# A token norm's shift carried by the first scatter of each layer, and half of its gain moved to GpSimd

## The chip, the cores and the metric

The kernel runs on one core of one Trainium2 chip. The metric is the device time of one execution in microseconds. The engines go by the names of the profile: PE is TensorE (PEld its weight loads), DVE is VectorE, ACT is ScalarE, POOL is GpSimd, SP is SyncE, which here only issues DMAs. An engine's name with a q behind it is its sequencer.

## The reference

Two layers, each with four token mixers, a projection, a norm, a mixture of 16 experts with two experts for each token, and a second norm. There are 256 tokens of 2048 values; everything is float32. What the change touches is the path from the first norm of a layer to the sum over the experts:

```python
h = layer_norm(DN_ALPHA * h + mix, ln1_g[l], ln1_b[l])
ffn = hier_moe(h, w_rg[l], b_rg[l], w_re[l], b_re[l], w_gate[l], w_up[l], w_down[l])
h = layer_norm(DN_ALPHA * h + ffn, ln2_g[l], ln2_b[l])

...
for e in range(N_EXPERTS):
    h = jax.nn.silu(xt @ w_gate[e]) * (xt @ w_up[e])
    out = out + combine[:, e:e + 1] * (h @ w_down[e])
```

The loop stands in `hier_moe`, where `xt` is `h` as 256 x 2048. `combine` is zero for all but the two experts that the router picks for a token, so only those have to be computed.

## The kernel before

The tokens lie in SBUF as `h`, 128 partitions by two halves (`h[:, 0]`, `h[:, 1]`) by 2048. After the output projection VectorE normalises each half without gain and shift. TensorE turns it and computes the router's logits; gain and shift are folded into the router's weights there. Then VectorE picks the experts for each token, counts the tokens of each expert, and gives every expert one or more blocks of 32 token places (BLK). Experts are sorted by their number of blocks, the fixed first two (FIXED) ahead; the sorted table goes as whole numbers into `tabi`, from which each engine loads registers to set its loops. The part for the first two experts is written first, and signalled as `tab_first`; the rest follows later, as `tab_ready`.

A block runs so. VectorE makes `hot`, a matrix that marks which token fills which place (function `mark`; for the first block it signals `first_hot`). TensorE gathers the rows of `h_k`, a copy of the normalised tokens that ScalarE made (`hk_ready`), and turns them (L1010); VectorE applies gain and shift in `take_rows` and signals `xe_ready`. TensorE multiplies with the gate and up weights (L1038). ScalarE and VectorE form the hidden values (`sgate`, `hidden`), TensorE turns them and multiplies with the down weights (L1056). The result `yraw` is scattered back onto the tokens by a product with `place`, a matrix of 0 and combine weight (L1021, `scatter`), and VectorE adds the scattered banks to `h` (`add_block`). The scatter of a block is done one block later: in block g TensorE scatters block g - 1, four banks for the first half of the tokens, behind the gather of the next block, and four for the second half behind the first half of the down products. It may write a bank again only when VectorE has added it. So the first block of a layer has a scatter with nothing to carry: `place` is set to zero for it (L1576), and it adds zeros.

Since `h` holds the normalised tokens until the gather has its copy, VectorE multiplies both halves by the gain (L1555, L1556, signal `gain_done`) between the first `mark` and the table, and adds the shift to both (L1581, L1582) before the loop over the blocks. Gain and shift come as `gb`, each vector broadcast to 128 partitions by SyncE, 1 MB each, once the mixed heads are split (`mix_split`); they end as the signal `gb1_loaded`. The rows that say where each token goes, `rows`, lie over the gain in memory, so ScalarE's copy into `rows` (L714) waits for `gain_done`.

Behind these two loads SyncE issues the expert weights: six units of 2 MB for an expert (four of gate and up, two of down), into nine slots of SBUF. A unit from the tenth on waits until the unit that held its slot has been used: `gu_quarter` after a quarter of the gate and up products of the last block of an expert, `gu_done`, `y_half` and `y_done` after the others. Unit 12 also waits for `tab_ready`. Each engine runs its instructions in the order in which they stand; nothing is rescheduled. GpSimd has no work between the entry norm's gain and shift (L489, L492, on `h`, while the mixers run) and the next layer.

In memory `area(48, ...)` begins with `yraw` (2 KB), `place` and `place_2` (1 KB each) and `rows` (4 KB).

Of the kernel before, what the change touches and what calls it, by code (L numbers as in the profile page):

```python
# [14 lines left out]
P = 128  # L15
BLK = 32
# [29 lines left out]
def trunk(nc, x, ln0_g, ln0_b, w_in, conv_a_w, conv_a_b, lru_wa, lru_ba, lru_wx, lru_bx, lru_lam, conv_b_w,  # L46
# [27 lines left out]
    with ctx:  # L74
# [67 lines left out]
        gb = area(48, 2 * D).rearrange("p (m n) -> p m n", m=2)  # L142
# [65 lines left out]
        table_by = yraw.rearrange("p (r e n) -> p r e n", r=2, e=16)  # L208
# [79 lines left out]
        gain_done, hk_ready = signal("gain_done", 1), signal("hk_ready", NT)  # L288
# [38 lines left out]
        def _(eng):  # L327
# [48 lines left out]
            for l in range(L):  # L376
# [20 lines left out]
                for m, v in enumerate((ln1_g, ln1_b)):  # L397
                    eng.dma_start(gb[:, m, :], v[l:l + 1].to_broadcast([P, D])).then_inc(gb1_loaded.sem, 16)
# [58 lines left out]
        def _(eng):  # L457
# [36 lines left out]
            for l in range(L):  # L494

                eng.wait_ge(xnT_done, (l + 1) * 8)
                eng.memset(c_scT, 0.0).then_inc(sc_zero.sem, 1)

                eng.wait_ge(bias_loaded.sem, bias_loaded.at(l, 16))
                eng.memset(blocks(a_H, HEADS)[0:CH, :, 0:CH], NEG).then_inc(mask_ready.sem, 1)  # L500
                eng.wait_ge(gb_in_loaded, 32 * (l + 1))
                eng.wait_ge(w_used.sem, w_used.at(l, 21))
                affine(gb_in)


        @block.scalar
        def _(eng):
# [55 lines left out]
            for l in range(L):  # L563
# [148 lines left out]
                eng.wait_ge(gain_done.sem, gain_done.at(l, 1))  # L712
# [393 lines left out]
        def _(eng):  # L1106
# [104 lines left out]
            for l in range(L):  # L1211
# [343 lines left out]
                tt(h[:, 0, :], h[:, 0, :], gb[:, 0, :], ALU.mult)  # L1555
                tt(h[:, 1, :], h[:, 1, :], gb[:, 0, :], ALU.mult).then_inc(gain_done.sem, 1)  # L1556
# [9 lines left out]
                for r0, r1 in ((0, 2), (2, 3)):  # L1566
                    n = r1 - r0
                    tt(table_by[:, 0:n], tab[:, r0:r1].rearrange("p r (o e) -> p r o e", o=1).to_broadcast([P, n, 16, 16]),
                       sorted_by.rearrange("p (o n) e -> p o n e", o=1).to_broadcast([P, n, 16, 16]), ALU.mult)
                    eng.drain()  # L1570
                    eng.tensor_reduce(tabf[:, r0:r1], table_by[:, 0:n], AX.X, ALU.add)
                    eng.drain()
                eng.tensor_copy(tabi[:, 0:3, FIXED:], tabf[:, :, FIXED:])
                tt(tabi[:, 3, FIXED:], tabf[:, 0, FIXED:], tabf[:, 1, FIXED:], ALU.add).then_inc(tab_ready.sem, 1)
                eng.wait_ge(spread_ready.sem, spread_ready.at(l, 1))
                eng.memset(place, 0.0).then_inc(place_ready, 1)  # L1576
# [3 lines left out]
                tt(h[:, 0, :], h[:, 0, :], gb[:, 1, :], ALU.add)  # L1580
                tt(h[:, 1, :], h[:, 1, :], gb[:, 1, :], ALU.add)  # L1581
# [69 lines left out]
```

## Time and profile before

| | us |
|---|---|
| median of 3 runs | 1740.17 (1737.57 to 1743.55) |
| the profiled execution, its time | 1737.94 |
| the profiled execution, its span | 1736.2 |
| TensorE busy | 1578.6 (91%) |
| VectorE busy | 922.2 (53%) |
| ScalarE busy | 522.3 (30%) |
| GpSimd busy | 48.8 (3%) |
| mean DMA rate | 315 GB/s |

The span is what the profiler covers, from the first to the last instruction of one execution; the time of that execution is 1.7 us longer. A layer takes about half of the span: some 410 us of mixers and router, then some 450 us of experts. The page gives busy time and, in slices, how it is spread; a timeline gives the start and length of each instruction and, in brackets, how long its engine stood idle before it and what ended that. Windows give the busy time of each engine between two moments, in the order PE, PEld, DVE, ACT, POOL, with the granted clock of TensorE as a share of 2.4 GHz, the share of time in which the DMA engines were busy, and GB/s. Most of VectorE's instructions come through two helpers and so have the line L1108 or L1111.

### The profile page before, as it was taken

What the parts mean: (1) busy time and instruction counts of PE and PEld (TensorE: products, weight loads), DVE (VectorE), ACT (ScalarE), POOL (GpSimd) and SP (SyncE); (2) the same over time, 40 slices, a digit from 0 to 9 for tenths busy, and PEclk for the clock granted to TensorE, in tenths of its full rate; (3) what the DMA queues carried; (4) which work ended last, traced back from release to release, by engine and by line L of the source; (5) the groups of instructions that cost most, each with busy time, mean ns of one, the idle gap of its engine ahead of it and who ended that gap; (6) DMA issues with size and microseconds to landing.
All of it is one profiled execution on the core that took longest, in us unless ns stands there. A gap on an engine that the chain in (4) does not pass through costs nothing.

```text
span 1736.2 us, 35349 instructions
## 1 busy us (share of the span) xinstructions
PE 1578.6 (91%) x14820; PEld 1067.3 (61%) x14821; DVE 922.2 (53%) x1443; ACT 522.3 (30%) x600; POOL 48.8 (3%) x34
## 2 busy tenths in 40 slices
PE   8999999997999999956699999999989999996664
PEld 8999899884444444322299999998754444432221
DVE  7657655646455555422467476455465455543234
ACT  4553453323121121110264543543232121211011
POOL 0004000000000000000000050000000000000000
PEclk9999999999999999988899999999989999998887
DMA  9554455588999999999965545555989999999996
GB/s 309 196 168 136 153 169 192 194 334 365 421 422 422 418 419 399 423 422 422 409 211 181 161 142 170 174 174 192 421 338 420 422 422 421 408 423 421 423 421 270
DMA packets 139206, 547.28 MB, mean 315 GB/s; under 512 B 23060, under 2 KB 26360, under 8 KB 88568
## 3 DMA queue, kind: packets, MB, share of 16 engines
q1 hardware_dynamic: 138740, 546.13, 80.7%
q8 instruction: 57, 0.93, 0.2%
q14 instruction: 21, 0.17, 0.0%
q10 hardware_dynamic: 388, 0.04, 0.0%
HBM read 544.04 MB, written 2.10 MB: 315 GB/s over the span
## 4 chain that ended last, share of the span: by engine, by line
PE 74%; SPq 15%; DMA 4%; DVE 3%; issue 2%; DVEq 1%; ACT 1%; ACTq 0%
PE ps L798 24%; PE ps L1038 14%; PE ps L955 10%; SPq L430 9%; PE ps L1056 7%; SPq L434 5%; PE ps L795 5%; PE ps L1021 4%; PE ps L1002 3%; DMA room<-in_w_down_dram 3%; PE ps L1010 1%; DVE room L1108 1%; DVE h L1108 1%; PE ps L874 0%; DMA h<-in_x_dram 0%
## 5 line engine op out<-in xcount | busy, mean ns | idle before, releaser
L1038 PE MATMUL ps<-room 128*32 128x256 f32 x6016 | 374.4, 407 | 95.7 <-DMA room<-in_w_up_dram 90.3
L1108 DVE TENSOR_TENSOR w_lo<-room,w_hi 128x2048 fp32r<-128x2048 f32 x120 | 276.8, 2316 | 237.3 <-ACT w_hi L513 236.8
L1038 PEld LDWEIGHTS ps<-room 128*32 128x32 f32 x6016 | 202.3, 116 | 283.0 <-DMA room<-in_w_up_dram 110.4
L798 PE MATMUL ps<-hT_hi,w_hi 128*128 128x256 f32 x1152 | 330.2, 287 | 1.6 <-DVE hT_lo L1108 1.6
L798 PE MATMUL ps<-hT_hi,w_lo 128*128 128x256 f32 x1152 | 327.2, 284 | 0.0
L798 PE MATMUL ps<-hT_lo,w_hi 128*128 128x256 f32 x1152 | 327.1, 284 | 0.0
L513 ACT ACTIVATE w_hi<-room 128x2048 fp32r<-128x2048 f32 x120 | 228.3, 1914 | 228.1 <-PE ps L798 103.8
L1108 DVE TENSOR_TENSOR h<-h,ps 128x512 f32<-128x512 f32 x376 | 232.7, 680 | 98.3 <-PE ps L1021 97.8
L798 PEld LDWEIGHTS ps<-hT_hi,w_hi 128*128 128x128 f32 x1152 | 222.4, 193 | 4.4 <-DVE hT_lo L1108 2.0
L798 PEld LDWEIGHTS ps<-hT_hi,w_lo 128*128 128x128 f32 x1152 | 222.4, 193 | 0.7 <-issue 0.5
L798 PEld LDWEIGHTS ps<-hT_lo,w_hi 128*128 128x128 f32 x1152 | 222.3, 193 | 0.0
L1108 DVE TENSOR_TENSOR room<-room,ps 128x128 f32<-128x128 f32 (+2 forms) x53 | 18.5, 352 | 368.4 <-ACT room L720 363.0
L1056 PE MATMUL ps<-room 128*32 128x512 f32 x1504 | 184.3, 608 | 10.8 <-DMA room<-in_w_down_dram 10.8
L709 ACT ACTIVATE room<-ps 128x512 f32<-128x512 f32 (+1 forms) x143 | 70.4, 492 | 369.1 <-PE ps L1056 261.0
L720 ACT ACTIVATE room<-ps 128x128 f32<-128x128 f32 x47 | 13.0, 277 | 367.1 <-PE ps L1038 367.1
L1021 PE MATMUL ps<-room 32*128 32x512 f32 x752 | 115.0, 642 | 6.5 <-DVE h L1108 5.3
L1056 PEld LDWEIGHTS ps<-room 128*32 128x32 f32 x1504 | 39.7, 110 | 114.0 <-issue 86.3
L955 PE MATMUL ps<-w_hi,mix_hi 128*128 128x512 f32 x256 | 100.0, 391 | 0.0
L955 PE MATMUL ps<-w_lo,mix_hi 128*128 128x512 f32 x256 | 99.6, 389 | 0.0
L955 PE MATMUL ps<-w_hi,mix_lo 128*128 128x512 f32 x256 | 99.6, 389 | 0.0
L1002 PE MATMUL ps<-room 128*32 128x512 f32 x784 | 94.4, 599 | 2.5 <-DVE room L1108 2.5
L1021 PEld LDWEIGHTS ps<-room 32*128 32x128 f32 x752 | 34.0, 182 | 87.4 <-DVE h L1108 46.7
(246 smaller groups left out, 1421.3 us busy)
## 6 DMA issues: line engine op xcount, KB each, us to landing
room<-in_w_gate_dram SPq DMA_DIRECT2D x128, 1024.0 KB, 18.2
room<-in_w_up_dram SPq DMA_DIRECT2D x128, 1024.0 KB, 20.2
room<-in_w_down_dram SPq DMA_DIRECT2D x128, 1024.0 KB, 15.7
room<-in_w_in_dram SPq DMA_DIRECT2D x88, 1024.0 KB, 5.0
room<-in_w_out_dram SPq DMA_DIRECT2D x32, 1024.0 KB, 5.0
room<-in_ln_g_dram SPq DMA_DIRECT2D x5, 1024.0 KB, 5.6
room<-in_ln_b_dram SPq DMA_DIRECT2D x5, 1024.0 KB, 8.0
h<-in_x_dram SPq DMA_DIRECT2D x4, 512.0 KB, 6.3
```

Of the source, the lines that this page charges most:

```text
L430: eng.dma_start(unit_gu(u)[:, m], src[:, 4 * i:4 * i + 4, :]).then_inc(unit_loaded[u % SLOTS], 16)
L434: eng.dma_start(unit_down(u)[:, f, :], src[:, 2 * (i - 4) + f, :]).then_inc(unit_loaded[u % SLOTS], 16)
L513: eng.activation(w_hi[n % 4][:], w_raw(n % UNITS), ACT.Copy).then_inc(w_rounded.sem, 1)
L709: eng.activation(dst, ps[:, b, 0:dst.shape[1]], ACT.Copy).then_inc(ready, 1)
L795: last = eng.matmul(ps[:, b + o, :], x_[:, kk, o * P:o * P + P], w_, start=opens, stop=ends)
L798: last = eng.matmul(ps[:, b + o // 2, (o % 2) * T:(o % 2) * T + T], w_[:, o * P:o * P + P], x_[:, kk, :], start=opens and o % 2 == 0, stop ...
L955: last = eng.matmul(ps[:, b + t, :], m[:, k, t * P:t * P + P], w, start=(q == 0 and k == 0 and j == 0), stop=(q == 3 and k == 3 and j == 2))
L1002: last = eng.matmul(ps[r0:r0 + BLK, 3, :], hot[:, t, :], h_k[:, t, 4 * c:4 * c + 4, :], start=(t == 0), stop=(t == NT - 1), tile_position= ...
L1021: eng.matmul(ps[:, 4 + c, :], place[r0:r0 + BLK, t * P:t * P + P], yraw[r0:r0 + BLK, :], start=True, stop=True, tile_position=(r0, 0)).the ...
L1038: last = eng.matmul(ps[r0:r0 + BLK, 0, 0:2 * P], xe[:, x0:x0 + BLK], unit_gu(u)[:, :, k, c * P:c * P + P], start=(i == 0 and k == 0), stop ...
L1056: last = eng.matmul(ps[r0:r0 + BLK, 2, :], hmT[:, BLK * f:BLK * f + BLK], unit_down(u)[:, f % 2, c * 512:c * 512 + 512], start=(f == 0), s ...
L1108: return eng.tensor_tensor(o, a, b, op)
```

## The change

In each layer:

- `gb` becomes `gain_1`, the gain alone, and lies elsewhere (area 56). The shift is no longer broadcast: it is loaded as four rows of 512 values into `yraw`, at partitions 0, 32, 64 and 96, after GpSimd has set `yraw` to zero (signal `yraw_zero`). SyncE waits for that before it issues the load.
- `place` is set by VectorE to 1 where the partition's number within its 32 is 0 (`slot_of`), and 0 elsewhere, in place of zeros throughout. So the first scatter adds the shift to every token, and the two adds of the shift on VectorE go.
- The gain of `h[:, 1]` moves from VectorE to GpSimd, which waits for `gb1_loaded`, `hk_ready` and `first_hot`. `gain_done` now comes from GpSimd, and VectorE waits for it before the loop. ScalarE's copy into `rows` no longer waits for it.
- `place` is set right behind the gain of `h[:, 0]`, so the wait for `spread_ready` (that copy's signal) moves ahead of the table. The table's scratch is now `place_2`, half as large, so its three rows are computed one by one and not two and one.

The diff, cut; behind the two lines of memory come SyncE's part, GpSimd's, ScalarE's and VectorE's:

```diff
-        gb = area(48, 2 * D).rearrange("p (m n) -> p m n", m=2)
+        gain_1 = area(56, D)
...
-        table_by = yraw.rearrange("p (r e n) -> p r e n", r=2, e=16)
+        table_by = place_2.rearrange("p (r e n) -> p r e n", r=1, e=16)
...
                 eng.wait_ge(mix_split.sem, mix_split.at(l, 4))
-                for m, v in enumerate((ln1_g, ln1_b)):
-                    eng.dma_start(gb[:, m, :], v[l:l + 1].to_broadcast([P, D])).then_inc(gb1_loaded.sem, 16)
+                eng.dma_start(gain_1, ln1_g[l:l + 1].to_broadcast([P, D])).then_inc(gb1_loaded.sem, 16)
+
+                eng.wait_ge(yraw_zero.sem, yraw_zero.at(l, 1))
+                eng.dma_start(yraw[0:P:BLK, :], ln1_b[l].rearrange("(c n) -> c n", c=4)).then_inc(gb1_loaded.sem, 16)
...
                 affine(gb_in)
+                eng.wait_ge(mix_split.sem, mix_split.at(l, 4))
+                eng.memset(yraw, 0.0).then_inc(yraw_zero.sem, 1)
+
+                eng.wait_ge(gb1_loaded.sem, gb1_loaded.at(l, 32))
+                eng.wait_ge(hk_ready.sem, hk_ready.at(l, NT))
+                eng.wait_ge(first_hot.sem, first_hot.at(l, 1))
+                eng.tensor_tensor(h[:, 1, :], h[:, 1, :], gain_1, ALU.mult).then_inc(gain_done.sem, 1)
...
-                eng.wait_ge(gain_done.sem, gain_done.at(l, 1))
                 eng.wait_ge(spread_done.sem, spread_done.at(l, 1))
...
-                tt(h[:, 0, :], h[:, 0, :], gb[:, 0, :], ALU.mult)
-                tt(h[:, 1, :], h[:, 1, :], gb[:, 0, :], ALU.mult).then_inc(gain_done.sem, 1)
+                tt(h[:, 0, :], h[:, 0, :], gain_1, ALU.mult)
+                eng.wait_ge(spread_ready.sem, spread_ready.at(l, 1))
+
+                ts(place, slot_of[:].to_broadcast([P, T]), 0.0, None, ALU.is_equal).then_inc(place_ready, 1)
...
-                for r0, r1 in ((0, 2), (2, 3)):
+                for r0, r1 in ((0, 1), (1, 2), (2, 3)):
...
-                eng.wait_ge(spread_ready.sem, spread_ready.at(l, 1))
-                eng.memset(place, 0.0).then_inc(place_ready, 1)
...
-                tt(h[:, 0, :], h[:, 0, :], gb[:, 1, :], ALU.add)
-                tt(h[:, 1, :], h[:, 1, :], gb[:, 1, :], ALU.add)
+                eng.wait_ge(gain_done.sem, gain_done.at(l, 1))
```

On GpSimd, in the first layer from the clearing of `c_scT` for the mixers to the same instruction of the second layer; before:

```order
L497 MEMSET room 128x1024 [waits xnT_done]
L500 MEMSET room 64x4x64 [waits bias_loaded]
L489 TENSOR_TENSOR h<-h,room 128x2048 [waits w_used,gb_in_loaded]
L489 TENSOR_TENSOR h<-h,room 128x2048
L492 TENSOR_TENSOR h<-h,room 128x2048 x2
L497 MEMSET room 128x1024 [waits xnT_done]
```

and of the changed kernel:

```order
L499 MEMSET room 128x1024 [waits xnT_done]
L502 MEMSET room 64x4x64 [waits bias_loaded]
L491 TENSOR_TENSOR h<-h,room 128x2048 [waits w_used,gb_in_loaded]
L491 TENSOR_TENSOR h<-h,room 128x2048
L494 TENSOR_TENSOR h<-h,room 128x2048 x2
L507 MEMSET room 128x512 [waits mix_split]
L512 TENSOR_TENSOR h<-h,room 128x2048 [waits first_hot,hk_ready,gb1_loaded]
L499 MEMSET room 128x1024 [waits xnT_done]
```

Two instructions are new there, and the second is released by VectorE's `first_hot`.

On VectorE, from the gain to the table's end in the first layer (`room` is the memory in which nearly all tiles lie, `place` and the table among them); before:

```order
L1108 TENSOR_TENSOR h<-h,room 128x2048 [waits hk_ready,gb1_loaded]
L1108 TENSOR_TENSOR h<-h,room 128x2048
L1557 COPY room<-slot_of 128x1
L1108 TENSOR_TENSOR carry<-carry,room 128x1
L1560 TENSOR_REDUCE room<-room 128x16
L1561 COPY room<-iota 128x16
L1108 TENSOR_TENSOR room<-room,iota 128x256
L1108 TENSOR_TENSOR room<-room 128x512
L1571 TENSOR_REDUCE room<-room 128x32
L1108 TENSOR_TENSOR room<-room 128x256
L1571 TENSOR_REDUCE room<-room 128x16
```

and of the changed kernel:

```order
L1116 TENSOR_TENSOR h<-h,room 128x2048 [waits hk_ready,gb1_loaded]
L1119 TENSOR_SCALAR room<-slot_of 128x256 [waits spread_ready]
L1567 COPY room<-slot_of 128x1
L1116 TENSOR_TENSOR carry<-carry,room 128x1
L1570 TENSOR_REDUCE room<-room 128x16
L1571 COPY room<-iota 128x16
L1116 TENSOR_TENSOR room<-room,iota 128x256
L1116 TENSOR_TENSOR room<-room 128x256
L1581 TENSOR_REDUCE room<-room 128x16
L1116 TENSOR_TENSOR room<-room 128x256
L1581 TENSOR_REDUCE room<-room 128x16
```

The second gain has become the small instruction that makes `place`, and the table's pair of instructions of 512 has become two pairs of 256; one more pair of 256 follows in the changed kernel.

Further on, from the table's end to the loop's first add; before:

```order
L1573 CAST tabi<-room 128x3x14
L1108 TENSOR_TENSOR tabi<-room 128x14
L1576 MEMSET room 128x256 [waits spread_ready]
L309 TENSOR_LOAD tabi [waits tab_first]
L309 ISA x2
L309 TENSOR_LOAD tabi
L309 ISA x2
L1539 REGISTER_ALU
L1108 TENSOR_TENSOR room<-room,ps 128x128 [waits sg_ready]
L1108 TENSOR_TENSOR h<-h,room 128x2048 x2
L1583 UNCONDITIONAL_BRANCH
```

and of the changed kernel:

```order
L1583 CAST tabi<-room 128x3x14
L1116 TENSOR_TENSOR tabi<-room 128x14
L309 TENSOR_LOAD tabi [waits tab_first]
L309 ISA x2
L309 TENSOR_LOAD tabi
L309 ISA x2
L1547 REGISTER_ALU
L1116 TENSOR_TENSOR room<-room,ps 128x128 [waits sg_ready]
L1590 UNCONDITIONAL_BRANCH [waits gain_done]
```

The two adds of 128x2048 and the memset are gone, and the wait for `gain_done` stands where the adds stood.

## Rows read from the trace of the kernel before

**Rows 1.** Page, parts 1 and 2: TensorE's busy time; DMA in 40 slices.
```profile
PE 1578.6 (91%) x14820; PEld 1067.3 (61%) x14821; DVE 922.2 (53%) x1443; ACT 522.3 (30%) x600; POOL 48.8 (3%) x34
...
GB/s 309 196 168 136 153 169 192 194 334 365 421 422 422 418 419 399 423 422 422 409 211 181 161 142 170 174 174 192 421 338 420 422 422 421 408 423 421 423 421 270
```

**Rows 2.** Windows of the expert stages; last columns clock, DMA share, GB/s.
```profile
420.00:590.00 170.00, 165.17 (x2055) 71.89 (x2047) 92.32 (x197) 33.79 (x55) 0.00 (x0) 0.98 1.01 421
590.00:700.00 110.00, 109.09 (x1400) 47.69 (x1398) 59.63 (x131) 21.22 (x35) 0.00 (x0) 1.00 1.00 411
700.00:850.00 150.00, 103.45 (x1137) 41.15 (x1137) 46.68 (x103) 17.04 (x27) 0.00 (x0) 0.89 1.01 422
1280.00:1450.00 170.00, 165.21 (x2027) 70.97 (x2023) 92.54 (x196) 31.64 (x54) 0.00 (x0) 0.98 1.01 421
1450.00:1530.00 80.00, 79.15 (x1021) 34.70 (x1017) 44.31 (x96) 16.63 (x27) 0.00 (x0) 1.00 1.01 415
```

**Rows 3.** Windows of two holes; SyncE's issue that ends the first.
```profile
413.00:418.00 5.00, 4.49 (x60) 3.58 (x64) 3.50 (x6) 0.46 (x1) 0.00 (x0) 1.00 0.14 54
...
690.00:692.00 2.00, 2.00 (x44) 1.23 (x40) 0.40 (x3) 0.00 (x0) 0.00 (x0) 1.00 0.64 147
...
417.88 0.33 SPq L430 DMA_DIRECT2D room<-in_w_gate_dram  x1
```

**Rows 4.** Timelines around first_hot: start, duration, engine, instruction; PEldq: register loads.
```profile
410.51 0.22 DVE L1108 TENSOR_TENSOR room<-hot 128x64 f32<-128x64 f32 x1
...
410.90 0.24 DVE L1111 TENSOR_SCALAR room<-room,carry 128x16 f32<-128x16 f32 x1
...
411.36 0.16 DVE L1108 TENSOR_TENSOR tabi<-room 128x2 int32<-128x2 f32 x1
...
411.50 0.15 DVE L1507 SCALAR_TENSOR_TENSOR tabi<-room,carry 128x1 int32<-128x1 f32 x1
...
L309 PEldq SEQ_ASSERT  x2: 18/21/24, 412.5 to 413.1; - x2
...
413.51 0.66 PE L1010 MATMUL ps<-ident,room 128*128 128x128 f32 x4 [0.71 <-ACT room L709]
...
415.89 7.11 PE L1038 MATMUL ps<-room 128*32 128x256 f32 x128
...
1270.24 0.66 PE L1010 MATMUL ps<-ident,room 128*128 128x128 f32 x4 [0.71 <-ACT room L709]
```

**Rows 5.** Timelines of the first block; last row from the chain.
```profile
416.40 4.49 DVE L1108 TENSOR_TENSOR h<-h,room 128x2048 f32<-128x2048 f32 x2
...
426.49 4.49 DVE L1108 TENSOR_TENSOR h<-h,room 128x2048 f32<-128x2048 f32 x2
...
431.99 3.60 PE L1021 MATMUL ps<-room 32*128 32x512 f32 x8 [2.74 <-DVE h L1108]
...
439.16 7.83 PE ps L1038 x128
```

**Rows 6.** VectorE beside GpSimd, timelines; first two groups of instructions (ns).
```profile
L1108 DVE TENSOR_TENSOR w_lo<-room,w_hi 128x2048 fp32r<-128x2048 f32 x120 | 276.8, 2316 | 237.3 <-ACT w_hi L513 236.8
...
L489 POOL TENSOR_TENSOR h<-h,room x4: 4506/5024/5559, 152.7 to 1012.5; 128x2048 f32<-128x2048 f32 x4
...
154.40 3.88 DVE L1310 SCALAR_TENSOR_TENSOR room<-room 128x1024 f32<-128x1024 f32 x1
...
162.84 4.61 POOL L492 TENSOR_TENSOR h<-h,room 128x2048 f32<-128x2048 f32 x1
...
163.70 5.90 DVE L1108 TENSOR_TENSOR w_lo<-room,w_hi 128x2048 fp32r<-128x2048 f32 x1 [5.41 <-ACT w_hi L513]
```

**Rows 7.** Windows at the lower clock; an idle stretch, timeline.
```profile
434.00:440.00 6.00, 6.00 (x31) 1.46 (x33) 5.20 (x13) 0.75 (x2) 0.00 (x0) 0.51 1.02 423
1291.00:1297.00 6.00, 6.00 (x35) 1.42 (x36) 4.95 (x13) 1.01 (x2) 0.00 (x0) 0.50 1.01 418
...
397.95 2.07 PE L924 MATMUL ps<-ident,h 128*128 128x128 f32 x16 [2.18 <-DVE h L1111]
```

More of the change, by code:

```diff
@@ L287, in trunk @@
             signal(n, 1) for n in ("logits_done", "ex_in", "ex_ready", "m_ready", "ranks_done", "tab_ready"))
-        gain_done, hk_ready = signal("gain_done", 1), signal("hk_ready", NT)
+        yraw_zero, gain_done, hk_ready = signal("yraw_zero", 1), signal("gain_done", 1), signal("hk_ready", NT)
         spread_done, spread_ready, wts_ready = (signal(n, 1) for n in ("spread_done", "spread_ready", "wts_ready"))
```

## The prediction

> **What bounds the kernel now.** I read the page first, in 40 slices: TensorE is busy nearly everywhere, and DMA moves about 420 GB/s through the two long expert stretches (slices 11 to 20 and 31 to 39) [rows 1]. The windows of these stretches say more. From 420 to 590 us, and again from 700 to 850, the DMA engines deliver 421 and 422 GB/s without a hole, while TensorE is 97% and 69% busy; between them, from 590 to 700, they deliver 411 [rows 2]. The second layer shows the same: 421, then 415 between 1450 and 1530. So the expert stage is bound by the stream of weights. Its length is the moment at which the stream restarts, plus the bytes, plus the holes in the stream. I look for what moves the restart, and what fills the holes.
>
> *The restart.* From 413 to 418 us DMA is all but idle (54 GB/s) [rows 3]: all nine slots are full, and the next load waits until the first expert's first quarter of gate and up products releases one. SyncE issues it at 417.88 [rows 3]. TensorE begins these products at 415.89 [rows 4]. A microsecond that this start slips is a microsecond of the DMA bound stage.
>
> *The holes.* At 690 to 692 us DMA is down to 147 GB/s [rows 3]. In this part an expert has two blocks of tokens and TensorE takes a little longer for one than the stream does, so slots come free late. Holes in the first layer: (422 - 411) / 422 x 110 us = 2.9 us. In the second: (422 - 415) / 422 x 80 us = 1.3 us. Together 4.2 us. That is all that an earlier TensorE can win in both layers: after 700 us it waits for weights anyway.
>
> **What the change takes away.** After the first gate and up products VectorE has two gains (416.40, 4.49 us) and later two shifts (426.49, 4.49 us), 2.25 us each; TensorE's second scatter of the first block waits for the adds behind them, until 431.99, idle for 2.74 us [rows 5]. Afterwards TensorE runs at the lower of its two clocks, granted 0.51 from 434 to 440 us [rows 7]. The change removes both shifts and one gain from VectorE. Count from G, the start of the gate and up products (415.89 before [rows 4]). The product of the hidden layer, just ahead of the shifts, ended at 426.5, G + 10.6 [rows 5]. It comes 2.25 us sooner for the gain, and about 0.5 us later for the third pair of small instructions that the table now takes: G + 8.9; the mask of ones costs what the zeros cost. The loop's first four adds then wait for the first scatter alone and end, by an estimate of 0.7 us each, at about G + 12.1. TensorE stood before its second scatter at 431.99 - 2.74 = 429.25, G + 13.4; it gets there at G + 12.9, as its first scatter no longer waits half a microsecond for the mask behind the table. No wait is left. The second scatter (1.1 us) and the second half of the down products (1.9 us, half of what they take at the low clock) end at G + 15.9, where the second expert begins, instead of at G + 23.3 (439.16): 7.4 us earlier, of which 2.7 us is the wait and most of the rest the low clock.
>
> *How much arrives.* The next weights cap it. Units of 2 MB land 5 us apart from the restart on; counted so, the third expert has to wait some 2 us for its last down unit, and TensorE's lead over the stream is then about 5.6 us. That still exceeds the holes of either layer. I book the holes as filled: **-4.2 us**, and no more. The copy of the rows on ScalarE no longer waits for the gain: worth nothing by itself, as the mask is wanted only at G + 2.8. The megabyte less of broadcast shift is 2.4 us of DMA time ahead of a 5 us hole: nothing. The clearing of yraw on GpSimd is due when the mixed heads are split, long before SyncE's last load of projection weights; SyncE does not wait for it: nothing, at most 1 us, and that too before the hole.
>
> **What the change adds: GpSimd's gain, at a bad place.** GpSimd gets the factor for h[:, 1] as soon as first_hot is signalled, at 410.73. What do the two engines do to one another when both read two tiles from SBUF? The trace has the pair, where GpSimd applies the entry norm: its four products of this size take 4.51 us at the least and 5.56 at the most, and VectorE's scalar_tensor_tensor of 128x1024, issued at 154.40 in their midst, takes 3.88 us. VectorE's subtraction at 163.70 takes 5.90 us where the mean of its 120 fellows is 2.32: it ends at 169.60, just 2.15 us after GpSimd's instruction that began at 162.84 and took 4.61 ended (167.45) [rows 6]. So an instruction of either waits until the other's is over, whole, and the two don't share.
>
> Here VectorE has small work on the path at that time: the number of blocks of the first experts, written to tabi. At 411.36 comes a tensor_tensor of 128x2 with two SBUF operands [rows 4], two instructions short of tab_first at about 411.65. GpSimd starts at about 410.9 and holds to 410.9 + 4.5 = 415.4. tab_first then comes 0.3 us behind (if only the tensor_tensor is held) or 0.75 us behind (if the tensor_scalar at 410.90 is held too): 415.7 to 416.1, 4.0 to 4.5 us late. Behind it stand, on TensorE, two register loads (from tab_first to 413.1) [rows 4], and then the turning of the first rows, which began at 413.51 when ScalarE's copy released it: there 0.4 us of slack. So the turning starts at 417.1 to 417.6, and G with it 3.6 to 4.1 us later. I take 3.8. In the second layer the turning began at 1270.24 [rows 4] with 0.5 us of slack and slightly faster loads: 3.3 to 3.8, I take 3.5. Sum **+7.3 us**, all of it ahead of the restart. VectorE's own gain comes after GpSimd has finished, and gain_done is long there when the loop wants it.
>
> The Trainium skill has this as a rule ("SBUF — State Buffer", Who interferes with whom): the port pair shared by VectorE and GpSimd is an exclusive lock held for the whole instruction, and a VectorE instruction with two SBUF inputs contends with a GpSimd one that reads SBUF; the trace agrees, with its 5.90 us. The page adds that a tensor_scalar or a cast can take the pair in its two-port mode, by which the later end of my bracket would hold (0.45 us a layer more); that instructions of a few elements are held no run here shows yet.
>
> **The clock.** TensorE would idle from 412.8, the gather's end, to about 417.3, 4.5 us (before, 0.71 us stood here [rows 4]). The idle stretch of 2.74 us at the first scatter was followed by 6 us at half clock, and in the second layer there is the same fall at the same place [rows 5, 7]; an idle stretch of 2.18 us at 396 us was not followed by one. I expect the lower clock here in both layers, over the first quarter at least: 7.11 us for 128 products is 1.8 us a quarter, twice that at half clock, so 1.8 us a layer, **+3.6 us**. From below this is 0; from above it is half of 6.6 us of low clock, 3.3 us a layer. The later fall at 434 us goes, as its idle stretch goes; that is in the 7.4 us above.
>
> **Sum.** 7.3 + 3.6 - 4.2 = +6.7 us. The profiled execution took 1737.94 us, with a span of 1736.2; it would become 1744.6. The median of the three runs, 1740.17, is 2.2 us above it, and on that I forecast **1747 us**, 0.4% slower.
>
> **Rivals.**
> A, the forecast: held, low clock, holes filled. 1747 (1744 to 1751).
> B, held, but the clock stays at 2.4 GHz as it did at 396 us: 7.3 - 4.2 = +3.1, 1743.
> C, the other side: VectorE's small instructions slip through, or GpSimd starts only after 411.6. All rows of a hold concern 1024 elements and more. Then G stays and the holes are filled: -4.2, 1736. The point from which it decides is a hold of 2.1 us a layer: below it the change gains.
> D, held, and the holes stay, since the lower clock and the late landings eat the lead: 7.3 + 3.6 = +10.9, 1751.
> E, half a hold, since GpSimd has to wait its turn and finds VectorE between two instructions: about 0, 1740.
>
> **Chances.** A 0.50, B 0.20, C 0.14, D 0.08, E 0.08. A measurement of this kernel tells about 0.3% from no change, 5.2 us, so slower means above 1745.4 and faster below 1735.0. Slower: 0.40 of A, 0.03 of B, all of D: 0.51. Faster: 0.06 of C and 0.01 of E: 0.07. Within: 0.42. The range from 1738 to 1752 leaves out most of C below (0.11) and 0.05 above; the likeliest case's own is 1744 to 1751.
>
> **What would show it.** In the timeline after: GpSimd's product from about 410.9 for 4.5 us; VectorE's tensor_tensor on tabi lasting about 4 us instead of 0.16; the gate and up products from about 419.7 instead of 415.9; DMA idle for about 9 us, not 5; a granted clock near 0.5 in the quarter before the restart; no wait of TensorE at the second scatter; no hole between 590 and 700 us, and 422 GB/s there. I am wrong if tabi's instruction stays at 0.16 us (then C), or if the window from 590 to 700 still has 411 GB/s (then D).

## The result, and the profile after

The changed kernel takes 1745.76 us, the kernel before 1739.67 (medians of 13 runs each). The ratio is 1.0041, with a 95% interval of 1.0031 to 1.0052: slower by 0.4%. One run of the changed kernel (2250.70 us) and one of the kernel with 1024 columns further on (3902.77 us) stood far off from all others and count in no ratio. The profiled execution took 1745.64 us, its span is 1743.6, 7.4 us above the one before.

The page of the changed kernel, against [rows 1]:

```profile
PE 1575.7 (90%) x14820; PEld 1067.6 (61%) x14821; DVE 918.6 (53%) x1441; ACT 522.3 (30%) x600; POOL 58.8 (3%) x38
...
GB/s 308 195 178 130 164 174 175 193 343 282 421 421 422 421 422 416 422 422 421 408 201 179 170 140 161 168 188 194 385 311 421 422 422 421 422 422 422 422 422 276
```

The stream looks as before but for the slices at its restart (365 GB/s is now 282 in the first layer, 421 and 338 are now 385 and 311 in the second). The windows of the late part of each expert stage, against [rows 2] (the last number is GB/s):

```profile
590.00:700.00 110.00, 109.09 (x1403) 47.80 (x1395) 58.03 (x127) 21.50 (x36) 0.00 (x0) 1.00 1.01 419
...
1450.00:1530.00 80.00, 79.72 (x1016) 34.75 (x1009) 41.81 (x92) 16.04 (x28) 0.00 (x0) 1.00 1.01 422
```

The stream has 419 GB/s where it had 411, and in the second layer 422 where it had 415. The holes are filled, the first layer's not wholly: (422 - 419) / 422 x 110 us = 0.8 us is left. So the change brings nearly all that it could bring, and the loss comes from elsewhere. VectorE around first_hot, against [rows 4]:

```profile
411.34 0.17 DVE L1119 TENSOR_SCALAR room<-room 128x32 f32<-128x32 f32 x1
411.59 4.56 DVE L1119 TENSOR_SCALAR room<-room,carry 128x16 f32<-128x16 f32 x1
...
416.38 0.16 DVE L1116 TENSOR_TENSOR tabi<-room 128x2 int32<-128x2 f32 x1
...
416.51 0.15 DVE L1515 SCALAR_TENSOR_TENSOR tabi<-room,carry 128x1 int32<-128x1 f32 x1
```

and GpSimd in the same place:

```profile
411.60 4.53 POOL L512 TENSOR_TENSOR h<-h,room 128x2048 f32<-128x2048 f32 x1 [104.61 <-DVE room L1116]
```

VectorE's tensor_scalar of 16 elements, 0.24 us before, takes 4.56 us: it begins with GpSimd's product of 4.53 us and ends with it. tab_first is signalled behind the instruction at 416.51. TensorE and SyncE then:

```profile
418.39 1.11 PE L1018 MATMUL ps<-ident,room 128*128 128x128 f32 x4 [4.89 <-issue]
419.29 2.87 PE L1081 MATMUL ps<-ident,room 128*128 128x128 f32 x16
422.09 7.11 PE L1046 MATMUL ps<-room 128*32 128x256 f32 x128
...
434.47 1.20 PE L1029 MATMUL ps<-room 32*128 32x512 f32 x8
...
437.68 7.11 PE L1046 MATMUL ps<-room 128*32 128x256 f32 x128 [0.16 <-issue]
```

```profile
424.08 0.34 SPq L432 DMA_DIRECT2D room<-in_w_gate_dram  x1
```

TensorE stands idle for 4.89 us before it turns the first rows, for which it stood 0.71 us before. The gate and up products begin at 422.09, and the first weight is issued at 424.08. At the second scatter (434.47) it no longer waits. The granted clock (the column before DMA share) over the turning and the spreading of the places, in both layers:

```profile
418.00:421.00 3.00, 2.61 (x13) 2.62 (x13) 1.39 (x3) 0.00 (x0) 0.00 (x0) 0.50 0.02 5
...
1278.00:1281.00 3.00, 3.00 (x14) 3.00 (x15) 1.72 (x4) 0.00 (x0) 0.00 (x0) 0.50 0.03 5
```

From here on I count from the end of first_hot's instruction on VectorE, since that moment itself moves between executions (see the end). Restart is SyncE's first issue of a weight after the hole.

| from first_hot, us | before, layer 1 / 2 | changed, layer 1 / 2 |
|---|---|---|
| turning of the first rows | 2.78 / 2.77 | 6.96 / 6.58 |
| gate and up products (G) | 5.16 / 5.15 | 10.66 / 10.55 |
| restart of the stream | 7.15 / 7.14 | 12.65 / 12.54 |
| second expert, from the restart | 21.1 / 21.1 | 13.6 / 13.7 |
| last scatter of the stage | 449.4 / 448.2 | 452.6 / 452.7 |

The last scatter is TensorE's last instruction of an expert stage; before, and of the changed kernel, in both layers:

```profile
860.16 2.33 PE L1096 MATMUL ps<-room 32*128 32x512 f32 x16 [0.80 <-ACT room L709]
...
1715.67 2.32 PE L1096 MATMUL ps<-room 32*128 32x512 f32 x16 [0.80 <-ACT room L709]
```

```profile
864.06 2.32 PE L1104 MATMUL ps<-room 32*128 32x512 f32 x16 [0.80 <-ACT room L718]
...
1724.09 2.32 PE L1104 MATMUL ps<-room 32*128 32x512 f32 x16 [0.80 <-ACT room L718]
```

The stream restarts 5.5 and 5.4 us later. Less the filled holes, 2.1 and 1.3 us by the windows, that should leave 3.4 and 4.1 us; the stages are longer by 3.2 and 4.5. The 7.4 us between the spans are these two, 0.7 us by which first_hot itself came later in the first layer, and 1.0 us by which the second layer's last stretch, behind the last scatter, was shorter (19.5 against 20.5 us).

### The profile page after: what moved, and what is told of

The parts are those of the page before. It is cut to its first block, busy times and chain, and to the rows that moved or that the text cites. A ratio compares the mean times of both kernels' runs of the same rounds, so it can differ in the third digit from the quotient of the medians.

```text
span 1743.6 us, 35355 instructions
## 1 busy us (share of the span) xinstructions
PE 1575.7 (90%) x14820; PEld 1067.6 (61%) x14821; DVE 918.6 (53%) x1441; ACT 522.3 (30%) x600; POOL 58.8 (3%) x38
## 4 chain that ended last, share of the span: by engine, by line
PE 74%; SPq 14%; DMA 6%; DVE 3%; issue 2%; ACT 1%; DVEq 0%; ACTq 0%
PE ps L806 24%; PE ps L1046 14%; PE ps L963 10%; SPq L432 9%; PE ps L1064 7%; PE ps L803 5%; SPq L436 5%; DMA room<-in_w_up_dram 4%; PE ps L1029 4%; PE ps L1010 3%; DMA room<-in_w_down_dram 1%; PE ps L1018 1%; DVE room L1119 1%; PE ps L882 0%; PE ps L1055 0%
## 5 line engine op out<-in xcount | busy, mean ns | idle before, releaser
L1029 PE MATMUL ps<-room 32*128 32x512 f32 x752 | 109.7, 640 | 0.0
```

The source lines that it names most:

```text
L1029: eng.matmul(ps[:, 4 + c, :], place[r0:r0 + BLK, t * P:t * P + P], yraw[r0:r0 + BLK, :], start=True, stop=True, tile_position=(r0, 0)).the ...
```

## The experiments

**The change without GpSimd's part.** The gain of both halves on VectorE, all else as changed.

```diff
-                eng.tensor_tensor(h[:, 1, :], h[:, 1, :], gain_1, ALU.mult).then_inc(gain_done.sem, 1)
...
                 tt(h[:, 0, :], h[:, 0, :], gain_1, ALU.mult)
+                tt(h[:, 1, :], h[:, 1, :], gain_1, ALU.mult)
...
-                eng.wait_ge(gain_done.sem, gain_done.at(l, 1))
                 eng.drain()
```

> The changed kernel with the gain of both halves on VectorE; GpSimd has nothing to do near the expert stage. Let the restart be the time from the end of first_hot's instruction on VectorE to SyncE's first issue of an expert weight after the hole: 7.15 us before (417.88 - 410.73), 12.66 in the changed kernel (424.08 - 411.42). Theory H (GpSimd's instruction holds VectorE's small ones, and the stream of weights sets the stage's length): the restart is 7.2 us again in both layers, 590 to 700 us stands at 418 GB/s or more, and the time is 3 to 4 us below the kernel before, ratio 0.998. Rival S (the loss comes from the rest of the change: the shift's load, the scatter with ones, the longer table): the time stays about 6 us above the kernel before. Rival V (holes in the stream cannot be filled by an earlier TensorE): the time equals that of the kernel before, ratio 1.000.

1734.92 us, ratio 0.9983 (0.9970 to 0.9996): faster than both. TensorE's timeline:

```profile
413.49 0.66 PE L1014 MATMUL ps<-ident,room 128*128 128x128 f32 x4 [0.71 <-ACT room L714]
...
429.76 1.34 PE L1025 MATMUL ps<-room 32*128 32x512 f32 x8
```

The turning is back at 413.49 behind 0.71 us of idling, with no wait at the second scatter, and the restart is at first_hot + 7.14 in both layers. The windows at the same places as above, moved with first_hot:

```profile
589.98:699.98 110.00, 109.16 (x1403) 47.67 (x1395) 59.66 (x130) 21.24 (x35) 0.00 (x0) 1.00 1.01 419
1450.05:1530.05 80.00, 79.14 (x1037) 35.19 (x1033) 42.81 (x97) 16.16 (x26) 0.00 (x0) 1.00 1.01 421
```

The streams are those of the changed kernel, within 1 GB/s. The last scatters come 2.4 and 1.1 us sooner after first_hot than before, and the filled holes are 2.1 and 1.1 us. Theory H holds here, S and V fall: the scatter that carries the shift gains by itself, and the holes do get filled.

**GpSimd's part alone.** The kernel before, with the gain of `h[:, 1]` on GpSimd.

```diff
+                eng.wait_ge(first_hot.sem, first_hot.at(l, 1))
+                eng.tensor_tensor(h[:, 1, :], h[:, 1, :], gb[:, 0, :], ALU.mult).then_inc(gain_pool.sem, 1)
...
-                tt(h[:, 1, :], h[:, 1, :], gb[:, 0, :], ALU.mult).then_inc(gain_done.sem, 1)
```

> The kernel before with only the gain of h[:, 1] moved to GpSimd, released by first_hot; zeros scattered and shifts added on VectorE as before. Theory H: restart 12.7 us as in the changed kernel, 5.5 us more in each layer; VectorE has its two shift adds still, so TensorE's second scatter waits nearly as before and little of the holes is filled: +8 to +11 us against the kernel before, 3 to 5 us above the changed kernel. Rival (the moved gain is the gain of the change, and the shift does the harm): about 0.

1.0040 (1.0027 to 1.0053), +7 us. The restart is at 14.16 and 12.56 us, so the moved gain does the harm, as H says. (The execution profiled took 1752.86 us, 7.3 above the median. Its clock stayed low longer in the first layer: from the turning to the restart 7.2 us, where the changed kernel has 5.7 and the kernel before 4.4.) But I had expected 8 to 11, from holes that stay, and they do not stay: 418 and 422 GB/s. TensorE's wait at the second scatter is this short:

```profile
440.04 2.91 PE L1027 MATMUL ps<-room 32*128 32x512 f32 x8 [0.76 <-DVE h L1114]
```

One gain less on VectorE is enough to bring it from 2.74 to 0.76 us, and the second expert to 16.2 and 17.1 us after the restart, from 21.1. That is already more lead than the holes ask for. The shift's adds, on top of a gain moved away, cost next to nothing: the ratio is 1.0040 with them and 1.0041 without. So either half of the change alone fills the holes.

**How the loss goes with the length of GpSimd's product.** 512 and 1024 of the 2048 columns on GpSimd, the others on VectorE.

```diff
-                eng.tensor_tensor(h[:, 1, :], h[:, 1, :], gain_1, ALU.mult).then_inc(gain_done.sem, 1)
+                eng.tensor_tensor(h[:, 1, 1024:D], h[:, 1, 1024:D], gain_1[:, 1024:D], ALU.mult).then_inc(gain_done.sem, 1)
...
                 tt(h[:, 0, :], h[:, 0, :], gain_1, ALU.mult)
+                tt(h[:, 1, 0:1024], h[:, 1, 0:1024], gain_1[:, 0:1024], ALU.mult)
```

> The changed kernel with GpSimd's gain cut to 1024 of the 2048 columns of h[:, 1]; VectorE does the other 1024. Theory H: GpSimd's instruction takes about 2.3 us and VectorE's tensor_scalar with carry is held for all of it; the turning of the first rows comes 2.0 us later than before, counted from first_hot (2.78 us before, 6.97 changed, 4.75 here), the restart is about 9.2 us if TensorE keeps its clock and up to 10.5 if it falls; two layers of +2.0 to +3.3 against 4 us of filled holes: 0 to +3 us against the kernel before. Rival (any GpSimd product there costs a fixed amount, by its semaphores or a disturbed start): restart near 12.7 us, +6 us.

> As pool_1024, with 512 columns on GpSimd: an instruction of 1.2 us. Theory H: the turning at first_hot + 3.65 (2.78 before, 4.42 and 4.63 with 1024 columns, 6.97 with 2048), restart 8.0 us at full clock; 0.9 us for each layer against 3.4 us of filled holes: 1 to 2 us below the kernel before, ratio 0.999. Rival (a fixed cost of any GpSimd instruction there): restart of 8.8 us or more.

1.0008 (0.9995 to 1.0020) with 1024 columns, 0.9998 (0.9985 to 1.0011) with 512. VectorE's tensor_scalar with carry and TensorE's turning, with 1024 columns:

```profile
413.43 2.40 DVE L1119 TENSOR_SCALAR room<-room,carry 128x16 f32<-128x16 f32 x1
```

```profile
417.90 0.65 PE L1018 MATMUL ps<-ident,room 128*128 128x128 f32 x4 [2.57 <-issue]
```

| columns on GpSimd | GpSimd's product, us | turning from first_hot, layer 1 / 2 | restart, layer 1 / 2 | last scatter, layer 1 / 2 |
|---|---|---|---|---|
| 0 | none | 2.78 / 2.77 | 7.14 / 7.14 | 447.0 / 447.1 |
| 512 | 1.28 | 3.56 / 3.34 | 7.92 / 7.70 | 448.3 / 447.8 |
| 1024 | 2.37 | 4.63 / 4.42 | 10.61 / 8.79 | 450.7 / 448.8 |
| 2048 | 4.53 | 6.96 / 6.58 | 12.65 / 12.54 | 452.6 / 452.7 |

From 512 to 2048 columns the product grows by 3.25 us and the turning comes 3.40 and 3.24 us later: one for one. There is no fixed cost. With 1024 columns the restart is 1.8 us later in the first layer than in the second, although the turning differs by 0.2 only: that is the clock, which fell in one and not in the other (granted 0.68 from 418.3 to 421 us and 0.72 on to 424, against 1.00 from 1274 to 1277). It fell behind the turning and reached into the first quarter of the gate and up products. The point of no gain, which the prediction put at a hold of 2.1 us a layer, is in keeping with this. The times don't tell, as both ratios have 1 within their intervals; but against 449.4 and 448.2 before, the last scatters of both layers come 1.5 us sooner in sum with a product of 1.3 us, and 1.9 us later with one of 2.4. For 512 columns I had expected a time 1 to 2 us lower, which 0.9998 neither shows nor excludes.

**The same product, later.** GpSimd is released behind VectorE's first expert rows and next mark.

```diff
-                eng.wait_ge(first_hot.sem, first_hot.at(l, 1))
+                eng.wait_ge(late_go.sem, late_go.at(l, 1))
...
                 mark(hot_ready)
+                eng.drain().then_inc(late_go.sem, 1)
```

> The changed kernel with GpSimd's gain of the full half released only after VectorE has made the first expert rows and the next mark, by a new signal, and not by first_hot. Theory H: VectorE is held for 4.5 us again, but behind the start of the gate and up products: the restart is 7.2 us as before, the table and the hidden product come 4.5 us later than in the changed kernel, about G + 13.5, so that TensorE waits before the second scatter and its lead over the stream is some 3 us and not 7; holes are filled in part: 0 to -3 us against the kernel before. Rival (the hold costs the same wherever it lies): +6 us as in the changed kernel.

0.9983 (0.9969 to 0.9997), as without GpSimd's part. VectorE and GpSimd:

```profile
421.16 2.29 DVE L1117 TENSOR_TENSOR h<-h,room 128x2048 f32<-128x2048 f32 x1 [0.24 <-issue]
423.37 4.67 DVE L1120 TENSOR_SCALAR room<-slot_of 128x256 f32<-128x256 f32 x1
```

```profile
421.18 6.71 POOL L513 TENSOR_TENSOR h<-h,room 128x2048 f32<-128x2048 f32 x1 [111.36 <-DVEq L1561]
```

Here VectorE's gain was first, by 0.02 us in the record, and GpSimd's product stands behind it: 6.71 us, of which 4.5 is its own. Then VectorE's small mask of ones is held, 4.67 us. It is the same hold as in the changed kernel, and it costs the kernel nothing: restart at 7.14 in both layers, second expert at 19.0 us after it, last scatters 2.2 and 1.5 us sooner than before. The wait before the second scatter that I expected did not come. The place decides, not the work.

**The clock's share.** The changed kernel, with work for TensorE while VectorE is held.

```diff
                 gather(first_hot.sem, first_hot.at(l, 1), first_gathered.sem)
+                keep_busy(16, 7)
```

> The changed kernel with 16 products of the identity on TensorE between the gather of the first rows and the wait for tab_first, 4.0 us at full clock by 0.25 us each, so that TensorE is not idle while VectorE is held. Theory H with the clock's share: the hold stays (VectorE's tensor_scalar with carry 4.5 us, turning at first_hot + 7.0), but TensorE's clock does not fall before the gate and up products; the turning takes 0.66 and not 1.11 us, the spreading 1.95 and not 2.87; the restart is 11.3 us and not 12.65, in both layers: 2.6 us below the changed kernel, 3 to 4 us above the kernel before. Rival (the clock has no part in the loss, all of it is the hold): as the changed kernel, +6 to +7.

1.0026 (1.0014 to 1.0039), where the changed kernel has 1.0041. TensorE:

```profile
412.40 3.84 PE L773 MATMUL ps<-ident,ones 128*128 128x128 f32 x32
417.22 0.65 PE L1018 MATMUL ps<-ident,room 128*128 128x128 f32 x4 [0.97 <-issue]
417.70 1.95 PE L1082 MATMUL ps<-ident,room 128*128 128x128 f32 x16
```

The turning takes 0.65 us and the spreading 1.95; in the changed kernel they take 1.11 and 2.87. The restart is at 11.17 and 10.97 us, 1.5 and 1.6 us sooner. The last scatters come 1.4 and 1.8 us sooner too. So of the 5.5 us of delay in a layer some 1.5 are the lower clock, and 4.0 the hold. The two ratios alone would not show it, since their intervals overlap.

**Reads and writes.** The change without GpSimd's part, and GpSimd kept at work by five memsets, which only write.

```diff
+                eng.wait_ge(first_hot.sem, first_hot.at(l, 1))
+                for _ in range(5):
+                    eng.memset(rows.rearrange("p r t -> p (r t)"), 0.0)
+                    eng.drain()
+                eng.drain().then_inc(gain_done.sem, 1)
```

> shift_only, with GpSimd kept at work from first_hot on for about 5 us by five memsets of 128x1024 into the rows' place, which write SBUF and read nothing; ScalarE's copy into rows waits for them, as it did for the gain before. Theory H in the form that VectorE is held for its second way into SBUF by a GpSimd instruction that reads: restart 7.2 us, VectorE's small instructions at 0.15 to 0.25 us, the time of shift_only. Rival (any GpSimd instruction that touches SBUF holds VectorE's instruction in turn, reading or not): the tensor_scalar with carry takes about 1 us, the next ones as much in turns, tab_first 2 to 4 us late, +3 to +5 us against shift_only.

1.0001 (0.9987 to 1.0015). VectorE, with GpSimd's row below it:

```profile
415.60 0.87 DVE L1121 TENSOR_SCALAR room<-room,carry 128x16 f32<-128x16 f32 x1
415.75 0.73 DVE L1512 TENSOR_REDUCE room<-room 128x1 f32<-128x16 f32 x1
416.55 0.98 DVE L1514 CAST tabi<-room 128x4 int32<-128x4 f32 x1
416.63 0.91 DVE L1118 TENSOR_TENSOR tabi<-room 128x2 int32<-128x2 f32 x1
...
418.13 0.16 DVE L1118 TENSOR_TENSOR room<-room 128x2 f32<-128x2 f32 x1
```

```profile
415.49 5.23 POOL L510 MEMSET room<- 128x1024 f32 x5 [105.65 <-DVE room L1118]
```

Neither expectation was right. The tensor_scalar takes 0.87 us, until about the end of the first memset (five take 5.23 us); the cast at 416.55 takes 0.98, until about the end of the second. What is shown at 0.7 to 0.9 us behind each of them stands in the queue behind it and ends with it. But from 417.53 on, with GpSimd at work until 420.72, the two-operand tensor_tensor at 418.13 takes its usual 0.16 us. So a GpSimd instruction that only writes holds VectorE's tensor_scalar and cast, and not its tensor_tensor. The restart is at 8.04 and 7.92 us, 0.9 and 0.8 late. The second layer shows the same durations, row by row.

**Which instructions are held, and from what size.** The changed kernel with VectorE's small instructions in another order and one added.

```diff
-                ts(tab[:, 1, :], tab[:, 1, :], carry[:], None, ALU.add)
                 eng.tensor_reduce(total[:, 0, :], tab[:, 0, :], AX.X, ALU.add)
                 eng.drain()
+                tt(over[:, 0, 0:2], over[:, 1, 0:2], over[:, 2, 0:2], ALU.add)
+                eng.drain()
+                ts(tab[:, 1, :], tab[:, 1, :], carry[:], None, ALU.add)
+                eng.drain()
```

> The changed kernel with VectorE's instructions behind first_hot in another order: first the tensor_reduce of the total, then one added tensor_tensor of two elements with both operands in SBUF (on tile over, which is used up by then), then the tensor_scalar with carry. Theory H, by kind of instruction: the tensor_reduce has one SBUF operand and takes 0.16 us although GpSimd's product runs; the tensor_tensor of two elements is held until the product is over, 4 us and more; so the size of the held instruction has no part. Rival (only the kind of the tensor_scalar with carry is held, small tensor_tensors slip through): the added instruction takes 0.15 us and the tensor_scalar 4 us, as in the changed kernel.

1747.85 us in one run, with VectorE's timeline:

```profile
413.08 0.17 DVE L1509 TENSOR_REDUCE room<-room 128x1 f32<-128x16 f32 x1
413.32 4.31 DVE L1116 TENSOR_TENSOR over<-over 128x2 f32<-128x2 f32 x1
417.71 0.23 DVE L1119 TENSOR_SCALAR room<-room,carry 128x16 f32<-128x16 f32 x1
```

The tensor_reduce runs beside GpSimd's product (413.09 to 417.62) in 0.17 us. It is recorded 0.01 us before the product; but so is the tensor_scalar of the changed kernel, which was held. The tensor_tensor of two elements takes 4.31 us. The second layer shows the same two (0.17 and 4.30 us). Size has no part. Rival C of the prediction, that small instructions slip through, falls by this row.

**Is more lead worth more?** The first experiment, with half of one gain put into VectorE's wait for the first rows.

```diff
+                tt(h[:, 0, 0:1024], h[:, 0, 0:1024], gain_1[:, 0:1024], ALU.mult)
                 take_rows(first_turned.sem, first_turned.at(l, 1))
...
-                tt(h[:, 0, :], h[:, 0, :], gain_1, ALU.mult)
+                tt(h[:, 0, 1024:D], h[:, 0, 1024:D], gain_1[:, 1024:D], ALU.mult)
```

> shift_only, with the gain of 1024 columns of h[:, 0] put into the 1.7 us in which VectorE waits for the first rows to be turned; the hidden product then comes 1.2 us sooner. Theory C (the stream caps TensorE's lead at 2.5 us: counted from the restart, the fifth start of gate and up products lies at 50.3 and the sixth at 66.3 us in the changed kernel, in shift_only and in pool_late alike, against 52.8 and 68.8 before): starts at 50.3 and 66.3 again, and the time of shift_only, 0.998 of before. Rival (every microsecond that TensorE is earlier counts): the later starts 1.2 us sooner, the last hole of 0.8 us in the first layer gone, 1 us below shift_only.

0.9982 (0.9970 to 0.9994) against 0.9983: nothing more that the time could show. The starts on TensorE tell more. The second expert begins 14.2 us after the restart, where shift_only has 15.3, but the later starts are the same, 50.4 and 66.4 us after it. The start that lies at 66.3 in the other kernels, in TensorE's timeline of before and of the changed kernel:

```profile
486.65 5.60 PE L1038 MATMUL ps<-room 128*32 128x256 f32 x100 [0.56 <-issue]
```

```profile
490.33 1.93 PE L1046 MATMUL ps<-room 128*32 128x256 f32 x32 [0.56 <-issue]
```

486.65 - 417.88 = 68.8 before, 490.33 - 424.08 = 66.2 after. The lead of 7.5 us at the second expert has become 2.5, since TensorE catches up with the weights there. In this stretch of the changed kernel it waits 3.8 us for the third expert's gate and up units and then for its last down unit; before, it waited for none. pool_late comes to the second expert with 2.1 us of lead and waits for the last down unit alone, and is at 66.4 too. That wait in the changed kernel (in the weight loads) and in pool_late:

```profile
472.62 0.16 PEld L1064 LDWEIGHTS ps<-room 128*32 128x32 f32 x8 [0.97 <-DMA room<-in_w_down_dram]
```

```profile
471.25 1.92 PE L1065 MATMUL ps<-room 128*32 128x512 f32 x16 [0.56 <-DMA room<-in_w_down_dram]
```

These are 48.5 and 48.7 us after the restart. So the last down unit sets the cap. In all of them the first layer's late window has 418 or 419 GB/s, so a little of the holes is left whatever the lead was at first.

**A try at the clock further up.** shift_only, with seven products in TensorE's idle stretch of the router.

```diff
                 router(0)
+                keep_busy(7, 7)
```

> shift_only, with seven products of the identity (1.75 us at full clock) on TensorE in its idle stretch of 2.2 us between the two halves of the router. In the profiles so far first_hot ends at 410.4 to 415.4 us, later where the granted clock stands at 0.50 for some ten microseconds before it (404 to 411 us in the changed kernel, 1254 to 1266 us in the kernel before). Theory K (that idle stretch is what lets the clock fall, in some executions and not in others): the clock stays at 1.00 there, first_hot ends near 410.5 us in the first layer and the time is 1 to 4 us below shift_only, 0.996 to 0.998 of the kernel before, with less spread. Rival: the fall has another cause and comes as often as before, the time is that of shift_only, 0.998.

0.9979 (0.9965 to 0.9994): not to be told from 0.9983. The windows of the second layer's router and of the stretch from the turning of the first rows on, and TensorE's gather of the first rows ahead of that stretch:

```profile
1250.00:1266.00 16.00, 12.78 (x145) 11.04 (x144) 9.68 (x30) 8.47 (x7) 0.00 (x0) 1.00 1.01 425
1270.00:1276.00 6.00, 5.31 (x64) 3.42 (x60) 3.24 (x6) 2.13 (x3) 0.00 (x0) 0.85 0.05 19
...
1267.89 3.20 PE L1007 MATMUL ps<-room 128*32 128x512 f32 x16 [2.14 <-DVE room L1113]
```

Ahead of first_hot the clock stays at 1.00 in both layers (shift_only had 0.89 in this window of the second layer). But in the second layer it falls later, in the gather, which takes 3.20 us where shift_only has 1.92. The turning comes 4.04 us after first_hot and not 2.77, and the restart at 8.40 us and not 7.14; the turning and the gate and up products run at full clock again. One profile each doesn't settle whether the fall is only moved. And first_hot ends at 411.83 in the first layer, not near 410.5 as expected, since the router began later there (see the end). What the time says is that nothing clear is gained.

## Why the prediction was right, point by point

**The bound.** Right. The time follows the restart and the holes: +5.5 and +5.4 us of restart, less 2.1 and 1.3 us of holes, are 3.4 and 4.1 us; the stages grew by 3.2 and 4.5. The 0.4 us left over in the second layer is as much as the rounding of the windows (1 GB/s of 422 over 170 us is 0.4 us).

**The hold.** Right in mechanism and nearly in size. The turning came 4.2 and 3.8 us later; I had taken 3.8 and 3.5 from brackets of 3.6 to 4.1 and 3.3 to 3.8. The later ends were the right ones, and the first layer lies just beyond: the instruction held is the tensor_scalar with carry and not, as I expected to see, the tensor_tensor on tabi behind it. The sentence from the Trainium skill ("SBUF — State Buffer", Who interferes with whom), that a tensor_scalar or a cast can take the shared pair too, said so, and this trace (4.56 us) and the memsets (0.87 and 0.98 us) agree with it. The two elements (4.31 us) agree with the Trainium skill's rule for a VectorE instruction with two SBUF inputs, from the same section, which the prediction had. I should have taken the later end of the bracket. Counted from first_hot, tab_first came 4.3 us late in the first layer and the end of TensorE's register loads 4.5 (418.3 us, where it was 413.1); the slack took its 0.4 us off that.

**The clock.** Right in sign, its place wrong, its size 1.5 us a layer and not 1.8. I had put the low clock on the first quarter of the gate and up products. It fell at about 418 us and was back at 422.09, when they began; it fell on the turning and the spreading ahead of them, of which I had counted nothing. The size was partly luck, as it differs between executions: from the turning to the restart a layer took 4.4 us before, 5.7 and 6.0 in the changed kernel, and 7.2 and 7.1 in the first layers of pool_only and probe, where the low clock did reach into the first quarter. And what I held for rival B, an idle stretch of 2.18 us that no low clock followed, was one case of two in that trace: in the second layer the same stretch was followed by 12 us at 0.50 (1254 to 1266 us).

**What VectorE gains.** Right: the second expert begins at G + 15.6 (437.68 - 422.09), forecast G + 15.9, without a wait at the second scatter.

**The cap.** The step that failed in size: "TensorE's lead over the stream is then about 5.6 us. That still exceeds the holes of either layer". It is 2.5 us. I had taken the right unit, the third expert's last down unit, but put it about 3 us too early: a lead of 5.6 us would have the start that follows it at 47.2 us after the restart (52.8 before, less 5.6), and it is at 50.3. Why the unit lands so late is not shown. In the first layer 2.5 is less than the holes of 2.9, so a part stays, 0.8 us by the window, which has 419 GB/s, not 422. I booked 4.2 us for both layers; it is 3.4.

**The sum.** 8.0 for the hold (7.3 booked), 2.9 for the clock, the rest of the 10.9 us of restart (3.6 booked), and -3.4 for the holes (-4.2): +7.5 against a forecast of +6.7. The two stages grew by 7.7 us, the spans by 7.4, the medians by 6.1; first_hot's own moment moves by more than these differ from run to run. The path was right, the closeness of the sum is in part luck: the hold was booked 0.7 us too small and the clock 0.7 too large, which cancel, and the holes 0.8 too large. Of the rivals B falls, as the clock did fall, C and E as the hold is whole, and D as the holes did fill.

## What to carry to other kernels

Work moved to GpSimd is paid for in VectorE's time wherever VectorE's instructions of the held kinds run beside it, and the price is up to GpSimd's whole instruction, however small the held one is: 4.5 us for 16 elements here. So put it where VectorE's next instruction is on nobody's path (the same product, begun 5.8 us behind first_hot and not 0.2, cost nothing), or cut it short. And where a stream of weights sets a stage's length, an edit is worth what it does to the stream's restart and to its holes; lead beyond these is worth nothing, as 7.5 us of it became 2.5 here.

## What the runs showed of the hardware

- Held by a GpSimd product: VectorE's tensor_scalar, and its tensor_tensor down to two elements. Not held: tensor_reduce (0.17 us). Held by a GpSimd memset: tensor_scalar and cast, for the length of one memset; not held: tensor_tensor with both operands in SBUF (0.16 us).
- VectorE's gain that began 0.01 to 0.02 us before GpSimd's product was not held; the product waited for it (6.71 us in place of 4.53, in both layers). But the tensor_scalar of the changed kernel is recorded 0.01 us before the product in the first layer, and was held. Which of the two is first when they start so close together can't be read from the records.
- I had not expected first_hot's own moment to move as it does: in the first layer it ended between 410.4 and 415.4 us in these profiles, in kernels with nearly the same program up to there. Windows of the router in pool_late, where it ended at 415.41, and in the kernel before, at 410.73 (the clock is the third number from the end), each with TensorE's turning of the second half of `h` ahead of it:

```profile
404.00:408.00 4.00, 3.61 (x35) 3.16 (x28) 1.47 (x5) 2.76 (x2) 0.00 (x0) 0.50 1.02 426
...
398.69 3.68 PE L933 MATMUL ps<-ident,h 128*128 128x128 f32 x16 [2.18 <-DVE h L1120]
```

```profile
404.00:408.00 4.00, 3.06 (x27) 2.87 (x27) 3.25 (x17) 4.00 (x2) 0.00 (x0) 1.00 1.01 418
...
397.95 2.07 PE L924 MATMUL ps<-ident,h 128*128 128x128 f32 x16 [2.18 <-DVE h L1111]
```

The clock stood at 0.50 in the one and at 1.00 in the other. Both turnings follow the same idle stretch of 2.18 us. Over both layers of all the profiles but shift_fill's, the turning behind this stretch took 2.07 us in 7 of 22 cases, and first_hot then ended 12.6 to 12.8 us after its start; in the other 15 it took 2.5 to 3.7 us, and first_hot ended 13.8 to 16.7 us after. So one and the same idle stretch was followed by a lower clock in some executions and not in others, and that moves first_hot by up to 4 us. In shift_fill, with 0.5 us of idling, it took 2.07 us in both layers; two cases are few. The start of that turning moves too, from 395.9 us in the changed kernel to 399.1 in the first layer, which is why the changed kernel, with its clock at 0.50 as well, still ended at 411.43. Times counted from a mark inside the stage are free of this: the restart is at 7.14 or 7.15 us in both layers of all kernels in which GpSimd has no work at first_hot, but for shift_fill's second.
